# The last down projection of a two-layer encoder: 14 row tiles plain, eight row tiles as seven half-size products

## The reference, cut to what matters

```
def _swiglu(h, w_gate_up, w_down):
    gu = h @ w_gate_up                       # 512x1024 by 1024x5632
    return (silu(gu[..., :2816]) * gu[..., 2816:]) @ w_down     # f (512x2816) by w_down (2816x1024)

x = x + _swiglu(_rmsnorm(x, ffn_norm[1]), ffn_w_gate_up[1], ffn_w_down[1])
return _rmsnorm(x, final_norm)
```

## Time and profile before

| | us |
|---|---|
| median of 3 runs | 1260.75 |
| lowest, highest | 1260.67, 1260.84 |
| the profiled execution, its own time | 1260.39 |
| its span, first to last instruction | 1258.5 |
| PE busy of the span | 1248.9 (99%) |
| DVE, ACT, POOL busy | 833.5, 666.8, 400.8 |
| first matmul of the last down projection starts | 1124.34 |
| its last matmul starts | 1252.24 |

### The profile page before, as it was taken

How to read it: one execution, slowest core, us unless ns; L and a number is a source line. 1 busy time by engine, 2 the same in 40 slices (tenths; PEclk the granted TensorE clock), 3 DMA queues, 4 the chain that set the end, 5 groups by cost and what they waited for, 6 DMA issues and landing times.

```text
span 1258.5 us, 17761 instructions
## 1 busy us (share of the span) xinstructions
PE 1248.9 (99%) x6473; PEld 1001.3 (80%) x6473; DVE 833.5 (66%) x1324; ACT 666.8 (53%) x1240; POOL 400.8 (32%) x327
## 2 busy tenths in 40 slices
PE   9999999999999999999999999999999999999998
PEld 7877787777778888888888887677878888888886
DVE  3865766666636989898631146999898899872111
ACT  5554444444436765655532347786476655553233
POOL 4565663645625000000334443430210000024452
PEclk9999999999999999999999999999999999999999
DMA  6522222221144433420222335214452332122232
GB/s 188 198 70 64 66 67 59 64 65 56 58 139 142 152 126 109 134 99 3 93 82 86 101 102 191 84 58 151 127 183 102 134 103 68 65 76 85 84 100 92
DMA packets 102575, 126.60 MB, mean 101 GB/s; under 512 B 5976, under 2 KB 65624, under 8 KB 101848
## 3 DMA queue, kind: packets, MB, share of 16 engines
q1 hardware_dynamic: 102456, 125.45, 30.9%
q10 hardware_dynamic: 32, 0.01, 0.0%
HBM read 119.15 MB, written 6.29 MB: 100 GB/s over the span
## 4 chain that ended last, share of the span: by engine, by line
PE 89%; DVE 6%; issue 2%; ACT 2%; DMA 1%; POOL 0%; SPq 0%; POOLq 0%; DVEq 0%; ACTq 0%
PE ps L2100 26%; PE ps L2102 26%; PE ps L2101 26%; PE ps L2546 2%; PE ps L2459 2%; PE ps L2203 1%; PE ps L2215 1%; PE ps L2226 1%; PE ps L2261 1%; DMA w_stage<-in_even_w_out_dram 1%; PE ps L2238 1%; PE ps L2242 1%; DVE sq_sum L1358 1%; PE ps L2272 1%; PE ps L2280 1%
## 5 line engine op out<-in xcount | busy, mean ns | idle before, releaser
L687 POOL TENSOR_TENSOR w_lo<-w_stage,w_hi 128x512 fp32r<-128x512 f32 (+2 forms) x270 | 335.0, 1246 | 842.1 <-ACT w_hi L745 841.8
L745 ACT ACTIVATE w_hi<-w_stage 128x512 fp32r<-128x512 f32 (+2 forms) x288 | 163.8, 574 | 294.8 <-PE ps L2102 277.6
L2100 PE MATMUL ps<-h_hi,w_hi 128*128 128x512 f32 x464 | 190.2, 410 | 0.3 <-POOL w_lo L687 0.3
L2102 PE MATMUL ps<-h_hi,w_lo 128*128 128x512 f32 x464 | 181.3, 391 | 0.0
L2101 PE MATMUL ps<-h_lo,w_hi 128*128 128x512 f32 x464 | 181.2, 390 | 0.0
L2100 PE MATMUL ps<-w_hi,h_hi 128*128 128x512 f32 (+1 forms) x496 | 180.3, 363 | 0.2 <-DVE w_lo L1658 0.2
L2102 PE MATMUL ps<-w_hi,h_lo 128*128 128x512 f32 (+1 forms) x496 | 179.5, 362 | 0.0
L2101 PE MATMUL ps<-w_lo,h_hi 128*128 128x512 f32 (+1 forms) x496 | 179.3, 361 | 0.0
L2100 PE MATMUL ps<-w_hi,h_mix 128*128 128x512 f32 x320 | 125.2, 391 | 0.6 <-DVE w_lo L1658 0.5
L2102 PE MATMUL ps<-w_hi,h_mix 128*128 128x512 f32 x320 | 124.6, 389 | 0.0
L2101 PE MATMUL ps<-w_lo,h_mix 128*128 128x512 f32 x320 | 124.6, 389 | 0.0
(11 more groups left out here) (300 smaller groups left out, 2321.1 us busy)
## 6 DMA issues: line engine op xcount, KB each, us to landing
w_stage<-in_ffn_w_down_dram SPq DMA_DIRECT2D x88, 256.0 KB, 2.6
w_stage<-in_even_w_in_dram SPq DMA_DIRECT2D x96, 192.0 KB, 2.5
raw_c<-in_ffn_w_gate_up_dram SPq DMA_DIRECT2D x10, 1024.0 KB, 5.2
raw_b<-in_ffn_w_gate_up_dram SPq DMA_DIRECT2D x8, 1024.0 KB, 6.3
w_stage<-in_odd_w_in_dram SPq DMA_DIRECT2D x32, 256.0 KB, 2.7
w_stage<-in_ffn_w_gate_up_dram SPq DMA_DIRECT2D x6, 1024.0 KB, 5.4
raw_d<-in_ffn_w_gate_up_dram SPq DMA_DIRECT2D x6, 1024.0 KB, 7.2
raw_f<-in_ffn_w_gate_up_dram SPq DMA_DIRECT2D x6, 1024.0 KB, 5.4
```

The source lines that it names most:

```text
L687: pool.tensor_tensor(out=w_lo[:, s, 0:n], in0=stage[:, c % RING, :][:, 0:n], in1=w_hi[:, s, 0:n].bitcast(f32), op=ALU.subtract).then_inc(c ...
L745: act.activation(w_hi[:, s, 0:n], stage[:, s, 0:n], ACT.Copy).then_inc(chunk_hi, 1)
L2100: pe.matmul(out_, lh, rh, start=start, stop=False, skip_group_check=skip)
L2102: return pe.matmul(out_, ll, rh, start=False, stop=stop, skip_group_check=skip)
```

## The change

The 22 row tiles are parted. Fourteen (`PLAIN_TILES`) are multiplied as before, but for channels 512 to 1023 first and 0 to 511 second. The other eight (row tiles 2 to 9) form a 2x2 block product: tokens 0 to 255 and 256 to 511, rows 256 to 767 and 768 to 1279 of `w_down`, channels in two halves. It is done last, as seven products of four chunks with 6 matmuls each, in the order p1, p5, p6, p3, p7, p2, p4, into the PSUM banks beside or on top of the plain sums.

Matmuls: 2 x 14 x 12 = 336 plain ones and 7 x 4 x 6 = 168, together 504 instead of 528. The 18 turned tiles remain; four of them are turned in the second plain half. The eight block tiles are kept whole in `h_gained` (`pair_in`), split (`pair_high`, `pair_low`), and their sums made by `mix_sums`, `mix_high` and `mix_low` for j = 0 to 3. The weights of the block are loaded as four sets of 1 MB: two ahead of the down chunks, two behind chunk 5. Sixteen chunk sums of weights are made: eight on DVE (`down_sum`, p5 and p7) and eight on POOL behind its last `lo` (p6 and p3). The 28 `w_lo` of the products are made by DVE.

The end is reordered. Each of the eight half rows of y gets more than one addition (`y_add`, 20 in all, where there were 8 `y_sum`); token tiles 2 and 3 are complete before p2 and p4, and tiles 0 and 1 only after them. p4 runs one token tile after the other. The closing steps go in the order 2, 3, 0, 1.

The diff, cut to its core:

```diff
+PLAIN_TILES = (0, 1, 10, 11, 12, 13, 18, 19, 20, 21, 14, 15, 16, 17)
+NP = len(PLAIN_TILES)
+DOWN_PRODUCTS = ("p1", "p5", "p6", "p3", "p7", "p2", "p4")
...
 def low_by_dve(c):
-    return any(0 <= c - C_FFN[n] - GROUP_CHUNKS < UNIT_CHUNKS and (c - C_FFN[n]) % 4 < DVE_LOW_K for n in range(2))
+    return c >= unit_chunk(1, "p1", UNITS, 0) or any(0 <= c - C_FFN[n] - GROUP_CHUNKS < UNIT_CHUNKS and (c - C_FFN[n]) % 4 < DVE_LOW_K for n in range(2))
...
 # POOL, behind its last w_lo
+            for k in range(4):
+                pool.wait_ge(w_summed, summed_count(1, "p7", UNITS, k))
+                pool.wait_ge(raw_in["u2"][UNITS % 2], raw_loaded(1, UNITS))
+                pool.tensor_tensor(out=down_s2[:, k, :], in0=raw_tile(1, UNITS, "u2", k), in1=raw_tile(1, UNITS, "u1", k),
+                                   op=ALU.subtract).then_inc(last_summed, 1)
+            pool.wait_ge(chunk_used, C_FFN[1] + GROUP_CHUNKS + UNIT_CHUNKS + NP + 8)
+            for k in range(4):
+                pool.wait_ge(last_summed, k + 1)
+                pool.tensor_tensor(out=unit_source(1, "p3", UNITS, k), in0=raw_tile(1, UNITS, "g2", k), in1=down_s2[:, k, :],
+                                   op=ALU.subtract).then_inc(last_summed, 1)
...
 # ACT, from chunk NP + 9 of the plain ones
+                    for d in range(RING, 2 * NP):
+                        if d < NP:
+                            plain_high(d)
+                        conv(first + d)
...
+                        if d == NP + 9:
+                            pair_high(0)
+                            pair_in(2)
+                            pair_high(1)
+                            pair_high(2)
+                        if d == NP + 10:
+                            mix_high(2, 2)
+                        if d == NP + 11:
+                            pair_in(3)
+                            pair_high(3)
+                            mix_high(3, 2)
+                    for name in DOWN_PRODUCTS:
+                        for k in range(4):
+                            unit_high(n, name, UNITS, k)
+                            if name in ("p2", "p4") and k in (1, 2):
+                                y_square(int(name == "p4"), k + 1, 14 if name == "p2" else 16)
...
 # DVE
+                    for t in range(4, NP):
+                        plain_low(t)
+                    mix_sums(0, 2)
+                    mix_low(0, 2)
+                    mix_sums(1, 2)
+                    for c in range(NC):
+                        if c == 2:
+                            mix_low(1, 2)
...
+                        y_add(1, c, c)
+                    pair_low(0)
+                    pair_low(1)
+                    mix_sums(2, 2)
+                    pair_low(2)
+                    mix_low(2, 2)
+                    mix_sums(3, 2)
+                    pair_low(3)
+                    dve.wait_ge(f_turned, KF + NP + 8)
+                    for k in range(4):
+                        down_sum("p5", k)
+                    mix_low(3, 2)
+                    for k in range(4):
+                        down_sum("p7", k)
+                    unit_lows("p1")
+                    unit_lows("p5")
...
+                    unit_lows("p4")
+                    dve.wait_ge(gain_in, 16)
+                    dve.wait_ge(y_squared, 2)
+                    V.tensor_scalar(y_stat[:, 2, 2:4], y_stat[:, 0, 2:4], 1.0 / D, EPS, ALU.mult, ALU.add).then_inc(y_pre, 1)
+                    for c in (2, 3):
+                        y_gain(0, c)
+                    dve.wait_ge(y_gained, 2)
+                    y_finish(0, 2)
+                    dve.wait_ge(chunk_used, product_end(n, "p2", UNITS))
+                    for c in (0, 1):
+                        y_add(0, c, c)
+                    y_finish(1, 3)
+                    dve.wait_ge(y_summed, NC)
+                    y_add(1, 0, fb)
+                    dve.wait_ge(y_squared, 6)
+                    V.tensor_scalar(y_stat[:, 2, 0:2], y_stat[:, 0, 0:2], 1.0 / D, EPS, ALU.mult, ALU.add).then_inc(y_pre, 1)
+                    for c in (0, 1):
+                        y_gain(0, c)
+                    dve.wait_ge(y_gained, 4)
+                    y_finish(2, 0)
+                    dve.wait_ge(y_summed, NC + 1)
+                    y_add(1, 1, fb + 1)
+                    y_finish(3, 1)
...
 # the end of ACT's block
+            for i, c in enumerate((2, 3, 0, 1)):
+                if c == 0:
+                    y_square(0, 0, 17)
+                    y_square(0, 1, 18)
+                if c < 2:
+                    y_square(1, c, 19 + c)
...
 # TensorE
+                    for d in range(NP - 2):
...
+                        plain_down(0, d)
+                    turn_last(NP + 2)
+                    turn_last(NP + 3)
+                    plain_ends()
+                    for d in range(NP):
+                        if d in (6, 8):
+                            turn_last(NP + d - 2)
+                            turn_last(NP + d - 1)
+                        plain_down(1, d)
+                    for name in DOWN_PRODUCTS:
+                        down_multiply(name)
```

## The result

| us | before | after |
|---|---|---|
| median of 19 runs each | 1260.62 | 1262.81 |
| lowest, highest | 1259.96, 1261.45 | 1262.42, 1263.37 |
| profiled execution, its span | 1260.39, 1258.5 | 1263.37, 1261.6 |
| first matmul of the last down projection to its last (start to start) | 128.14 | 126.91 |
| last matmul's start to the end of the span | 6.26 | 10.08 |

The ratio is 1.0018, with an interval of 1.0012 to 1.0025: 2.2 us slower, a difference that shows outside its interval but lies just under the 0.2% that the prediction took as the bound of "the same". With 24 matmuls less, TensorE got through the stage 1.23 us sooner, and the end took 3.82 us more.

The account below looks back on a forecast made before the run. TensorE, busy 99% of the span, was taken as the bound. Matmuls -5.7, the end +3.9 and DVE's way to p1 +5.0 sum to +3.2 us: 1264.0 us against a median of 1260.75, range 1259.0 to 1266.5.

Parts of the forecast that it names:

- DVE late at p1, and six slow chunks: At p1's start: TensorE waits 2.9 us for DVE, then loses 0.35 for each of five chunks, 1.75 us.
- change of halves: Second plain half waits for `y_add` behind `mix_low(1, 2)`; late additions and TensorE restarts together cost 0.35 us.
- Part 1: Matmuls of the stage: 24 fewer save 5.44 us, an old wait 0.3, turned tiles unchanged; -5.7 us.
- Part 2: Behind the last matmul: DVE's list order makes the end 10.2 us instead of 6.26; +3.9 us.
- Part 3: DVE's way to p1: collisions with POOL make TensorE wait, then slow chunks and the change of halves; +5.0 us.
- U: Moment the second plain half's sixth chunk is used; TensorE wants p1 at U + 23.7, DVE's walk ends at U + 26.6.
- what would show it: Signs: wait of about 3 us before p1, five of 0.35 behind, POOL sums 1.7 us, DVE's 1.7 to 1.8.
- Part 4: Loads behind chunk 5 and POOL's sums for p6 and p3: in time, costing nothing.
- B: Rival at p1: DVE arrives in time, meeting POOL less or leaving the pair work earlier; 1259.3 us, chance 0.19.
- C: Rival at p1: only part is lost, slow chunks alone or a 1 to 2 us backlog; 1261.2 to 1262.7, chance 0.16.
- A: Forecast case: DVE and POOL take turns around p1's start; 1264.0 us, range 1262.7 to 1265.3, chance 0.52.
- D: Rival: DVE loses the whole 1.29 us per collision, 1267 us; beside it, a long wait might lower TensorE's clock; chance 0.10.

Follow-up runs that it names:

- e7: Changed kernel with POOL's eight sums moved to DVE, the end's lists reordered, and `mix_low(1, 2)` behind the four additions at the change of halves: 1256.03 us.
- e1: Changed kernel without POOL's eight weight sums, that computation left out (p6 and p3 read raw sets): 1258.57 us.
- e8: Kernel before the change with 24 of its plain matmuls in the second half left out: 1255.33 us.
- e3: Changed kernel with only the order of DVE's and ACT's lists at the end altered: 1260.47 us.
- e2: Changed kernel with all sixteen weight sums made on DVE, none on POOL: 1258.97 us.
- e5: Changed kernel with each of POOL's eight sums replaced by two fills, which read nothing: 1258.65 us.
- e9: Changed kernel with each of POOL's eight sums replaced by a copy of one SBUF operand: 1259.63 us.
- e4: Changed kernel with each of POOL's eight sums made twice: 1266.10 us.
- e10: Changed kernel with two p5 sums made a second time on DVE ahead of the last `mix_low`, so p1 starts later: 1264.96 us.

## Why the prediction was right, and where its terms were off

It was 1264.0 us; the median is 1262.81, in the range of 1262.7 to 1265.3 of the likeliest case, and slower than before, as forecast, though by less than the 0.2% from which I called it slower: by my own bounds it counts as the same, to which I had given 0.38 against 0.57. The span was predicted to 0.1 us (1261.7, measured 1261.6), partly by luck: the terms of this stage came to 0.6 less than I had summed, and the traced execution began the stage 0.5 later than that of before, for which I had no term and the runs show no cause.

| term | predicted | measured | from |
|---|---|---|---|
| TensorE without waits | -5.7 | -6.02 | stage of e7 against before |
| the end | +3.9 | +3.82 | 10.08 - 6.26 |
| DVE late at p1, and six slow chunks | +4.65 | +4.55 | stage of after against e1 |
| change of halves | +0.35 | +0.24 | stage of e1 against e7 |
| sum | +3.2 | +2.59 | |
| time ahead of the stage | 0 | +0.51 | 1124.61 - 1124.10 |

**Part 1** was 0.3 short. The 24 matmuls are 5.44 (e8) and the old wait is 0.33 (0.44 and 0.34 us from matmul to matmul, from 1243.05 on, instead of 2 x 0.2267). The rest is in the transposes: eight of the turned tiles are now transposed in pairs.

```profile
1159.01 1.03 PE L2708 MATMUL ps<-ident,f_tok 128*128 128x128 f32 x8
1159.80 0.47 PE L2345 MATMUL ps<-w_hi,f_home 128*128 128x512 f32 x1
```

Two chunks with a pair take 6.36 us (1186.36 to 1192.72) where their matmuls need 5.44, so a pair costs 0.92 instead of 2 x 0.49; four pairs give 0.24. Together this is 6.01 of the 6.02 measured. I had written that the turned tiles stay and cost the same.

**Part 2** holds link by link. With S = 1246.3, the start of p4's first matmul, the walk had the last addition at S + 9.6 = 1255.9 (1255.74), the last issue at S + 12.7 = 1259.0 (1258.86) and the end at 10.2 behind the last matmul (10.08). e3 shows that it was DVE's and ACT's order, and that most of it could be had back.

**Part 3** holds in kind and nearly in size. The walk itself is met. At its own pace TensorE would have begun p1 at 1209.14, which is U + 23.7, so U is 1185.4; the fourth `mix_sums` begins at U + 11.1 (1196.53) and p1 at U + 26.5 (1211.92), 2.8 us late, of which the profile counts 2.62 as idle. The walk's printed terms end at 20.2 + 0.7 + 5 x 1.1 = 26.4 and not at 26.6, since the 1.0 in the third `mix_sums` falls ahead of the U + 11.1; so it gave a wait of 2.7, and the 2.9 is a slip of 0.2. The trace has a wait of 2.62 instead of 2.9, six chunks with 1.73 instead of five with 1.75, POOL's sums at 1.7, DVE's at 1.70, all as written under what would show it. e1, e2, e5 and e9 show that POOL's reading is the cause and not DVE's amount of work: with the same work and eight sums more, DVE is in time. In e1 p1's first `w_lo` is ready 0.6 us before it is wanted. This is the 3.5 us of the prediction less the turns that e1 still has: 0.7 in the fourth `mix_sums` and 2.2 by POOL's last two `w_lo` (DVE's four p5 sums take 4.69 there too). In after three more turns, 3.3 us, fall from the p7 sums to the first `low`; 3.3 less 0.6 is the 2.7 of the walk. That a `y_add`, which reads one operand from PSUM, does not pay had no row ahead of the prediction; e4 shows it, where two of them beside POOL take 1.27 us, as two without POOL do in e1 (1.28).

**Part 4** stands: SP issues the two loads behind chunk 5 at 1125.21 and 1125.68, and no row of TensorE shows a wait at the seventh plain chunk.

**Of the rivals**, B (DVE in time, 1259.3) is what e1 and e2 measure without POOL's sums, 1258.6 and 1259.0: the rival was priced rightly, its condition was not met. C fell with the wait of 2.62; by the time alone it would hardly be told from A, for the median lies only 0.1 above its upper bound of 1262.7. D had each turn at the full 1.29: measured 1.09. A and D are parted by that length alone. D's second half, the clock, was nearer than its price said: I had reasoned that a wait of 2.9 would leave the clock at its high level and one well over 4 might not. It fell after 3.80, and once after 2.62. In after it did not, in the two traces taken.

**Against the medians** I was 1.2 us high, more than the span shows. The sum was 0.6 too high (3.2 for 2.59), and the base 0.1 (1260.75 of three runs, 1260.62 of 19). The other 0.4 is the distance from the 2.59 of the two traces to the 2.19 between the medians. Single executions lie that far from their medians: the one traced of before 0.23 us under, that of after 0.56 above, and the stage begins anywhere from 1123.70 to 1125.05 in the traces. I had used one execution of before as its base without that in the range; it is about as large as the smaller terms.

## What to carry to other kernels

An idle engine is not free when it shares a way to memory with the one that sets the pace: eight sums cost 0.60 us each on the busy DVE and nothing of the time, and 1.09 us of DVE each on the idle POOL, 4.55 us of the time in all. Ask of each added instruction on POOL what it reads and what DVE reads in the same microseconds, and whether DVE has a lead there; held back by some 3 us, the same sums cost 0.9. When work is taken from the last stage, walk the closing steps in each engine's own order again: here they cost 3.8 of the 6.0 us gained, and 2.75 of that was order alone.

## What the runs showed of the hardware that was not expected

- A collision of DVE and POOL has a length that goes with POOL's instruction: DVE loses 1.09 us to a 128x512 one with two fp32 operands in SBUF, 0.42 to a copy, nothing to a fill (after against e1, e9, e5). The two-operand turn is 0.2 us shorter than POOL's instruction alone, 1.29.
- Under steady collision each engine gets one instruction in about 1.7 us (e4: 6.80 to 6.88 us for four on DVE, 1.6 to 1.75 for one on POOL), where alone DVE takes 0.61 and POOL 1.29.
- A DVE addition with one operand in PSUM is not slowed by POOL: two of them take 1.27 us beside it (e4).
- In both traces in which TensorE's clock fell after a wait, it fell not in the wait but a little behind its end: in e10 the first six matmuls start 0.23 to 0.31 us apart before the step to 0.43, in e4 the first three. Whether it falls is not settled by the length of the wait alone: of four traces with 2.62 us one has the fall and three do not.
- Eight 128x128 transposes in a row take 0.79 us to the next matmul, four take 0.36 (1159.01 to 1159.80 in after, 1123.74 to 1124.10 in before). In all a pair of tiles costs 0.92 us and a single one 0.49; the rest of either, 0.13, is mostly the slower start of the matmul behind (0.32 us to the next instead of 0.23), which a pair pays once.
- Four output transfers of 256 KB issued back to back end 3.07 us behind the last issue, two end 2.7 behind it (e3, after; one trace each).
